# Residual of the last stage partly made by GpSimd, gate and scale applied in one step out of PSUM, last tile in halves

## The reference, cut to what matters

```python
xs = xs + g2s * _peer(h, ...)      # _peer ends in einsum('nhk,nhkd->nd', g * a, v_tab[e])
y_sample = _rmsnorm(xs, norm_final)  # xs * rsqrt(mean(xs*xs) + EPS) * norm_final
```

## Time and profile before

| | |
|---|---|
| median of three runs | 2218.42 us |
| profiled execution, its own time | 2221.55 us |
| its span, first to last instruction | 2219.6 us |
| granted TensorE clock, mean | 0.978 of full speed |
| PE busy | 2110.5 us (95%), 12150 instructions |
| DVE busy | 1781.8 us (80%), 3590 instructions |
| ACT busy | 1240.2 us (56%), 1677 instructions |
| POOL busy | 433.1 us (20%), 408 instructions |

### The profile page before, as it was taken

One profiled execution on the slowest core, in us unless ns is written; L12 is line 12 of the kernel. 1 busy time (PEld: TensorE's weight loads), 2 busy tenths in 40 slices (PEclk: granted clock), 3 DMA queues, 4 the chain that ended last, 5 costly groups with the idle time before them and its releaser, 6 DMA issues. The chain is left out here.

```text
span 2219.6 us, 33667 instructions
## 1 busy us (share of the span) xinstructions
PE 2110.5 (95%) x12150; PEld 1174.3 (53%) x12150; DVE 1781.8 (80%) x3590; ACT 1240.2 (56%) x1677; POOL 433.1 (20%) x408
## 2 busy tenths in 40 slices
PE   6999999978879999999999999999999999999997
PEld 3667676745557744445555554544444444444443
DVE  5467554776776668899999999935999999999999
ACT  4555863465767546524344457766556565565562
POOL 0011110000102200323232333400322222223220
PEclk8999998999999999999999999999999999999998
DMA  7975661008559645788999898995878888888872
GB/s 297 360 289 180 205 205 58 29 11 330 182 184 335 225 163 162 248 271 283 351 305 357 296 350 315 341 373 220 334 291 301 312 296 309 303 301 313 300 268 76
DMA packets 193531, 573.02 MB, mean 258 GB/s; under 512 B 18768, under 2 KB 52336, under 8 KB 186224
## 3 DMA queue, kind: packets, MB, share of 16 engines
q1 hardware_dynamic: 113728, 323.14, 42.4%
q0 software_dynamic: 48704, 173.04, 20.9%
q10 hardware_dynamic: 30960, 75.07, 8.7%
HBM read 454.18 MB, written 117.00 MB: 257 GB/s over the span
## 5 line engine op out<-in xcount | busy, mean ns | idle before, releaser
L307 PE MATMUL mrg_ps<-h_hi,lin_hi 128*128 128x512 f16 (+1 forms) x1376 | 462.2, 359 | 2.8 <-DVE h_lo L640 2.8
L307 PE MATMUL mrg_ps<-h_lo,lin_hi 128*128 128x512 f16 (+1 forms) x1376 | 462.1, 359 | 0.0
L307 PE MATMUL mrg_ps<-h_hi,lin_lo 128*128 128x512 f16 (+1 forms) x1376 | 461.8, 358 | 0.0
L2170 POOL DMA_INDIRECT row<-v_dram,picked x128 | 177.6, 1388 | 559.0 <-DVE acc L2812 438.0
L289 DVE SCALAR_TENSOR_TENSOR lin_lo<-lin_raw,lin_wsc,lin_hi 128x1024 f16<-128x1024 f32 x132 | 169.2, 1282 | 142.5 <-ACT lin_hi L283 142.4
L2234 POOL DMA_INDIRECT row<-u_rows_dram,picked x128 | 175.9, 1374 | 471.9 <-DVE dot_junk L2420 354.0
L283 ACT ACTIVATE lin_hi<-lin_raw,lin_wsc 128x1024 f16<-128x1024 f32 x132 | 151.1, 1146 | 199.5 <-DVE lin_wsc L144 158.2
L2682 PE MATMUL ps_w<-oh_turned,oh_buf 128*128 128x128 f16 x1024 | 224.3, 219 | 5.3 <-ACT region L2348 5.2
L307 PEld LDWEIGHTS mrg_ps<-h_hi,lin_lo 128*128 128x128 f16 x1376 | 135.3, 98 | 128.3 <-issue 1.4
L307 PEld LDWEIGHTS mrg_ps<-h_hi,lin_hi 128*128 128x128 f16 x1376 | 134.5, 98 | 120.5 <-issue 4.2
L307 PEld LDWEIGHTS mrg_ps<-h_lo,lin_hi 128*128 128x128 f16 x1376 | 135.3, 98 | 117.8 <-issue 1.1
(11 more groups left out here) (442 smaller groups left out, 3978.7 us busy)
## 6 DMA issues: line engine op xcount, KB each, us to landing
lin_raw<-w_all_dram SPq DMA_DIRECT2D x132, 512.0 KB, 6.1
act_scratch<-activated ACTq DMA_DIRECT2D x128, 256.0 KB, 4.5
wgt_scratch<-region ACTq DMA_DIRECT2D x64, 512.0 KB, 6.6
region<-v_dram SPq DMA_DIRECT2D x15, 2048.0 KB, 7.8
oh_buf<-v_dram SPq DMA_DIRECT2D x15, 2048.0 KB, 7.7
act_buf<-w_all_dram SPq DMA_DIRECT2D x38, 512.0 KB, 4.3
lin_hi<-split_scratch SPq DMA_DIRECT2D x64, 256.0 KB, 3.4
lin_lo<-split_scratch SPq DMA_DIRECT2D x64, 256.0 KB, 5.0
```

Of the source, the lines that this page charges most:

```text
L307: last = nc.tensor.matmul(self.ps[b % 2][:, half, 0:ts.stop - ts.start], w_[:, kc, :], x_[:, kc, ts], start=(j == 0 and kc == 0), stop=(j ...
L2170: nc.gpsimd.indirect_dma_start(out=row[j % NG][:], out_offset=None, in_=a["v"].rearrange("k (c d) -> (k c) d", d=D), in_offset=bass.Indire ...
```

## The change

GpSimd, after its last row fetch, makes `x2 + acc * gate` for the four latent tiles from the accumulator as it stands before the last group. For each tile it waits until that tile's two add-ups of the group before the last are done. VectorE's tail then handles a tile in two column halves: one step takes the last group's result from PSUM times the scale times the gate row (into `acc`), a second adds it to `x2`. Square sums are made in halves and added. The order of VectorE's tail changes: first half of tile k, variance and the four one-column steps of tile k-1, second half of tile k, normalisation of tile k-1; the last tile's normalisation and store go in two halves.

```diff
--- before.py
+++ after.py
@@ -2722,6 +2722,8 @@
             second.total_ps = pb(c, "ps_tot", [P, 2, 2])
             npass = VGROUPS // 2
             R = 2 * (NLAT // P)
+            BOTH = (slice(0, 512), slice(512, D))
+            FINAL = [(slice(0, D),)] * (NT - 1) + [BOTH]
             upto = [0] + [-(-PICKS * (g + 1) // (VGROUPS - 1)) for g in range(VGROUPS - 1)]
             block = c.enter_context(nc.Block())
 
@@ -2730,6 +2732,14 @@
                 for j in range(NG, PICKS):
                     pool.wait_ge(s("row_add"), j - NG + 1)
                     second_row(j)
+                pool.wait_ge(s("g2"), 4)
+                pool.wait_ge(s("ld7"), 16 * (NT + 1))
+                for k in range(1, NT):
+                    for r in (2 * k - 2, 2 * k - 1):
+                        pool.wait_ge(s(f"y_add{r % YB}"), (2 * R // YB) * (npass - 1) + r // YB + 1)
+                    nc.gpsimd.tensor_tensor(acc[:, k, :], acc[:, k, :], g2row[:, 1, :], ALU.mult).then_inc(s("base"), 1)
+                    pool.wait_ge(s("base"), 2 * k - 1)
+                    nc.gpsimd.tensor_tensor(x2[k][:, :], x2[k][:, :], acc[:, k, :], ALU.add).then_inc(s("base"), 1)
 
             @block.sync
             def _(sp):
@@ -2745,10 +2755,11 @@
                     sp.dma_start(x2[k][:, :], x2_d[k]).then_inc(s("ld7"), 16)
                 run(sp, 2, npass, step)
                 for k in range(NT):
-                    sp.wait_ge(s("final"), k + 1)
                     dst = y_prompt if k == 0 else y_sample[(k - 1) * P:k * P, :]
-                    sp.dma_start(dst, x2[k][:, :]).then_inc(s("st_y"), 16)
-                sp.wait_ge(s("st_y"), 16 * NT)
+                    for n, cs in enumerate(FINAL[k]):
+                        sp.wait_ge(s("final"), k + n + 1)
+                        sp.dma_start(dst[:, cs], x2[k][:, cs]).then_inc(s("st_y"), 16)
+                sp.wait_ge(s("st_y"), 16 * (NT + 1))
 
             @block.scalar
             def _(act):
@@ -2780,12 +2791,14 @@
                     act.wait_ge(s("fin_var"), k + 1)
                     nc.scalar.activation(st[:, 2, k:k + 1], st[:, 1, k:k + 1], ACT.Abs_reciprocal_sqrt).then_inc(s("fin_root"), 1)
                 for k in range(NT):
-                    act.wait_ge(s("resid"), k + 1)
-                    nc.scalar.activation(second.junk[:, 0:D], x2[k][:, :], ACT.Square, accum_out=st[:, 0, k:k + 1]
-                                         ).then_inc(s("ssq"), 1)
-                    act.wait_ge(s("ssq"), k + 1)
-                    if k:
-                        root(act, k - 1)
+                    for n, cs in enumerate(BOTH if k else FINAL[0]):
+                        done = 2 * k + n if k else 1
+                        act.wait_ge(s("resid"), done)
+                        nc.scalar.activation(second.junk[:, cs], x2[k][:, cs], ACT.Square, accum_out=st[:, 3 * n, k:k + 1]
+                                             ).then_inc(s("ssq"), 1)
+                        act.wait_ge(s("ssq"), done)
+                        if k and not n:
+                            root(act, k - 1)
                 root(act, NT - 1)
 
             @block.vector
@@ -2859,48 +2872,65 @@
                         for k in rows if r == R - 1 else (next(rows),) if r % 2 else ():
                             add_row(k)
 
-                def residual(k):
-
-                    if k == 0:
-                        dve.wait_ge(s("row_add"), PICKS)
-                        dve.wait_ge(s("g2"), 4)
-                        dve.wait_ge(s("ld7"), 16 * (NT + 1))
-                    else:
-                        for r in (2 * k - 2, 2 * k - 1):
-                            dve.wait_ge(s(f"y_add{(R + r) % YB}"), (2 * R // YB) * (npass - 1) + (R + r) // YB + 1)
-                    link(V.tensor_tensor(acc[:, k, :], acc[:, k, :], g2row[:, min(k, 1), :], ALU.mult))
-                    V.tensor_tensor(x2[k][:, :], x2[k][:, :], acc[:, k, :], ALU.add).then_inc(s("resid"), 1)
+                def residual_rows():
+
+                    dve.wait_ge(s("row_add"), PICKS)
+                    dve.wait_ge(s("g2"), 4)
+                    dve.wait_ge(s("ld7"), 16 * (NT + 1))
+                    link(V.tensor_tensor(acc[:, 0, :], acc[:, 0, :], g2row[:, 0, :], ALU.mult))
+                    V.tensor_tensor(x2[0][:, :], x2[0][:, :], acc[:, 0, :], ALU.add).then_inc(s("resid"), 1)
+
+                def residual(k, half):
+
+                    r, cs = 2 * k - 2 + half, BOTH[half]
+                    q = R + r
+                    dve.wait_ge(s("vp_y_inv1"), npass)
+                    dve.wait_ge(s("y_mm1"), R * (npass - 1) + r + 1)
+                    dve.wait_ge(s("base"), 2 * k)
+                    V.scalar_tensor_tensor(out=acc[:, k, cs], in0=ps_y[q % YB][:, :], scalar=second.yinv[:, 1:2],
+                                           in1=g2row[:, 1, cs], op0=ALU.mult, op1=ALU.mult).then_inc(s(f"y_add{q % YB}"), 1)
+                    dve.wait_ge(s(f"y_add{q % YB}"), (2 * R // YB) * (npass - 1) + q // YB + 1)
+                    V.tensor_tensor(x2[k][:, cs], x2[k][:, cs], acc[:, k, cs], ALU.add).then_inc(s("resid"), 1)
 
                 def variance(k):
-                    dve.wait_ge(s("ssq"), k + 1)
+                    dve.wait_ge(s("ssq"), 2 * k + 1)
+                    if k:
+                        link(V.tensor_tensor(st[:, 0, k:k + 1], st[:, 0, k:k + 1], st[:, 3, k:k + 1], ALU.add))
                     V.tensor_scalar(st[:, 1, k:k + 1], st[:, 0, k:k + 1], 1.0 / D, EPS, ALU.mult, ALU.add
                                     ).then_inc(s("fin_var"), 1)
 
-                def finish(k):
+                def inverse_root(k):
                     v_, root_, r_, t_ = (st[:, n, k:k + 1] for n in (1, 2, 3, 4))
                     dve.wait_ge(s("fin_root"), k + 1)
                     link(V.tensor_tensor(t_, root_, root_, ALU.mult))
                     link(V.tensor_tensor(t_, t_, v_, ALU.mult))
                     link(V.tensor_scalar(t_, t_, -0.5, 1.5, ALU.mult, ALU.add))
                     link(V.tensor_tensor(r_, root_, t_, ALU.mult))
-                    V.scalar_tensor_tensor(out=x2[k][:, :], in0=x2[k][:, :], scalar=r_, in1=nf[:],
-                                           op0=ALU.mult, op1=ALU.mult).then_inc(s("final"), 1)
+
+                def finish(k):
+                    for cs in FINAL[k]:
+                        V.scalar_tensor_tensor(out=x2[k][:, cs], in0=x2[k][:, cs], scalar=st[:, 3, k:k + 1], in1=nf[:, cs],
+                                               op0=ALU.mult, op1=ALU.mult).then_inc(s("final"), 1)
                 first_group()
                 for i in range(npass):
                     if i:
                         mixed(i, 0, i, 1)
                     if i < npass - 1:
                         mixed(i, 1, i + 1, 0)
-                residual(0)
+                residual_rows()
                 for k in range(1, NT):
-                    add_up(npass - 1, 1, 2 * k - 2)
-                    add_up(npass - 1, 1, 2 * k - 1)
-                    residual(k)
+                    residual(k, 0)
                     variance(k - 1)
+                    if k == 1:
+                        residual(k, 1)
+                    inverse_root(k - 1)
                     if k > 1:
-                        finish(k - 2)
+                        residual(k, 1)
+                    if k < NT - 1:
+                        finish(k - 1)
+                variance(NT - 1)
                 finish(NT - 2)
-                variance(NT - 1)
+                inverse_root(NT - 1)
                 finish(NT - 1)
 
             @block.tensor
```

## The result

| | before | after |
|---|---|---|
| median of the runs timed together | 2218.28 us (4 runs, 2216.62 to 2220.34) | 2234.44 us (4 runs, 2231.47 to 2238.45) |
| profiled execution / its span | 2221.55 / 2219.6 us | 2233.5 / 2231.7 us |
| granted TensorE clock, mean | 0.978 | 0.976 |
| VectorE busy | 1781.8 us, 3590 instructions | 1792.5 us, 3595 instructions |
| GpSimd busy | 433.1 us, 408 instructions | 458.0 us, 416 instructions |

The kernel became slower: ratio 1.0065, interval 1.0053 to 1.0077, which is +11.8 to +17.1 us. The forecast was +13.3 us (2231.7). The two spans differ by 12.1 us; in the profiled execution of after, everything ahead of the last stretch took 1.35 us less. So stretches are compared from a common anchor, the start of the last 2048-column multiply (line 485: 2166.77 before, 2165.42 after).

A forecast was written before the change was run, and what follows sets the result against it. VectorE's full queue was taken to bound the kernel's end. Holds of 13.55 us and -0.2 for the tail and store made +13.3: 2231.7 us for the median, own range 2223.6 to 2239, 8-in-10 range 2217.5 to 2239.

The forecast's parts named there:

- VectorE's queue is the tail: End of kernel: VectorE runs almost without pause from 2187.63 to 2216.58, so each microsecond it loses lengthens the kernel.
- Holds: VectorE from 2170.3: GpSimd's eight SBUF-reading instructions block its two-input steps and line 143, 13.55 us in all.
- the four that were to cost 1.62 behind an add-up: GpSimd instructions entering beside an add-up, holding the second split or a row step behind it: 6.48 us together.
- T: Length of one new GpSimd multiply or add of 128x1024: taken as 2.28 us, between 1.23 and 3.2.
- Who goes next: Back-to-back two-input VectorE steps: a waiting gather was said to wait for the second step too, taking 3.68 us.
- rival 1: VectorE beside GpSimd: its two-input steps go through and only GpSimd waits; -0.2 us, 2218.2; chance 0.24.
- rival 2: VectorE beside GpSimd: instructions interleave, about half the holds, +6.8 - 0.2, 2225.0; chance 0.08 together with rival 4.
- rival 4: Tail: GpSimd starts only there and VectorE waits for each base; +4, 2222; chance 0.08 together with rival 2.
- The tail: VectorE's tail in halves: 27.0 us against 26.55, +0.4, or -0.2 with gaps of 0.03; about 0.8 idle per tile.
- rival 3: Tail: no holds and no new idle time before the inverse root; up to 4 x 0.8 us saved, -3.4, 2215.0; chance 0.05.
- The store: End of kernel: the last store carries 256 KB instead of 512 and saves between nothing and half of 2.6; -0.6 taken.
- up to 6: TensorE before its last group: a hole of up to 6 us from holds ahead of its last split, costing nothing more.

The follow-up runs named there:

- the run with four: The changed kernel with GpSimd making only the four multiplies, not the four adds, against the kernel before: 2229.38 us, ratio 1.0048 (1.003 to 1.0067).

## Why the prediction was right

- **VectorE's queue is the tail.** It held: the +13.67 ahead of the first half, with the tail's +0.30 and the store's -0.5, came out at the end as +13.45. Nothing on the way swallowed it.
- **Holds, 13.55 forecast, 13.58 measured.** The total is nearer than its terms deserve. Line 143 lost 1.82 (1.95 forecast) and the first split 0.73 (0.78). Of the four that were to cost 1.62 behind an add-up, two cost 1.42, and two got in between back-to-back steps and cost 2.07 and 2.08. The residual lost 2.02 twice (2.17 forecast). T was 2.36 undisturbed and about 2.2 from the end of a blocking step, where 2.28 was taken. A held step doesn't begin anew when GpSimd is done: five of them end 1.08 to 1.09 us behind GpSimd's instruction, and not their length of 1.23 to 1.28. So most terms were too large and two too small, and that they cancel is luck. (The 0.33 between the row step's end and line 143 is 0.24 in the rows of both kernels.)
- **Who goes next was misread.** That a waiting gather lets a second back-to-back step pass was taken from the gather at 2124.70. Four others of before, at 1558.01, 1705.65, 1873.82 and 2041.45, also started during a row step with the multiply right behind it, and ended 0.81 to 0.82 behind the row step. Here is one, GpSimd's row and then VectorE's; its row step ends at 2042.57, the gather at 2043.38, and the multiply behind isn't held:

```profile
2041.45 1.93 POOL L2170 DMA_INDIRECT row<-v_dram,picked  x1 [0.92 <-DVE acc L2812]
```

```profile
2039.90 2.67 DVE L2812 SCALAR_TENSOR_TENSOR acc<-row,picked,acc 128x1024 f32<-128x1024 f32 x2
2042.48 2.28 DVE L485 TENSOR_TENSOR eq_buf<-eq_buf,sc_buf 128x2048 f32<-128x2048 f32 x1
```

So the holds of 2.07 and 2.08 could have been expected from the trace of before.
- **Only GpSimd waits (rival 1)** fails: the seven blocked instructions do wait, about 1 us each, but VectorE waits longer, and the kernel without them is at 1.001 (0.9997 to 1.0024). **Shared turns (rival 2)** fails in its price: 13.58 us for the eight where it had 6.8, and 8.02 for four alone. It is right in one thing, that VectorE's next step doesn't go first merely by standing ready.
- **GpSimd in the tail (rival 4)** isn't what happened, and its price of +4 was far too low. The run in which GpSimd starts only there loses as much as after: the prediction had priced VectorE's waits for the base, and not the holds that come with it there.
- **The tail: +0.4 forecast, +0.30 measured.** Idle times of 0.91, three of 0.82, and 0.79 stand where they were put (0.8 each). When the root is moved the three go, and 0.21 is left of the last (**rival 3** had the size right, 3.3 against the forecast 3.2 to 3.4, for another order than the kernel's). The 512-column add was 0.69 for a forecast 0.70; tile 1's 5.80 is as forecast. The gap behind the PSUM step was 0.03 to 0.04, not 0.11, and by the prediction that alone should have given its other end, -0.2. It didn't, in part because the sum holds the gap once in a tile and not twice: its second half runs from t+3.40 to t+4.85, 1.45 us where a half is 1.56.
- **The store:** -0.5 for -0.6. It landed in 2.1 us for 2.6. In the run without GpSimd's part the same half stores took 2.7, so this term is no sure gain.
- **TensorE** had a hole, 4.35 us for "up to 6"; the rest of the holds ahead of it was covered. The prediction left out the granted clock behind the hole. The windows of after show it (length, then PE, PEld, DVE, ACT, POOL busy, clock):

```profile
2184.00:2188.00 4.00, 0.47 (x2) 0.23 (x3) 4.00 (x4) 0.00 (x0) 2.11 (x2) 0.76 0.00 0
2188.00:2192.00 4.00, 4.00 (x11) 1.38 (x10) 4.00 (x3) 0.00 (x0) 3.92 (x2) 0.50 0.00 0
...
2196.00:2200.00 4.00, 4.00 (x20) 1.85 (x19) 3.96 (x2) 0.00 (x0) 3.92 (x2) 1.00 0.00 0
```

In 2188 to 2192 TensorE runs at 0.50, the lower of its two levels (1.2 GHz), with 11 matmuls instead of 20. It cost nothing here: VectorE is full in all these stretches, and at 2203.14 TensorE has waited 2.5 us for VectorE to give back a buffer.

What stays open is the difference of the medians, +16.2, to the +13.45 of the anchor. Single executions of after lie 7 us apart, and the interval (+11.8 to +17.1) holds both; the profiled executions can't say more, as the stretch ahead of the anchor was 1.35 us shorter in after's.

## What to carry to other kernels

An instruction that is given to GpSimd to relieve VectorE was free here only beside VectorE steps that take an operand from PSUM, or where VectorE had slack. So count its VectorE neighbours with two SBUF inputs, and charge each GpSimd instruction that reads SBUF up to its whole length against them (1.4 to 2.1 us of 2.36 where VectorE had no slack). One input is no safeguard: line 143 has one, and lost 1.82. If it must be there, cut it in pieces (8.05 us lost instead of 13.97). And when a tail is one engine's queue, look at where in the queue a result of another engine is first wanted: moving four small steps of each tile was worth 3.3 us in the trace here.

## What the runs showed of the hardware that was not expected

- A GpSimd multiply that comes while VectorE is in a two-input step starts before VectorE's next one, though that stands back to back: the second split and the row step behind lost 2.07 to 2.09 each time (after, and the run with four). Gathers of before did both: the one at 2041.45 got in behind the row step, and the one at 2124.70, which also started during a row step, ended 0.81 after the multiply that followed. Why these two differ wasn't tested.
- The hold doesn't depend on the held step's size. One-column steps of 0.16 with two SBUF inputs took 2.29 beside a GpSimd multiply and 2.00 beside an add, and the two-column line 143 took 1.99.
- Of the steps with one SBUF input, line 143 (two columns) was held, and the one-column step of line 2908 kept 0.15 at 2197.82, beside the add that started at 2197.65 (the run in which GpSimd starts late). What sets line 143 apart wasn't tested.
- A 256-column piece on GpSimd takes 0.72 us undisturbed, 2.9 for four by their sum, where one instruction of 1024 columns takes 2.36.
- A memset on GpSimd, which reads nothing, held line 143 to 0.54 from 0.17, while steps with two inputs, 1024 columns wide, lost nothing beside it.
- Four dependent one-column steps take 1.18 us on ScalarE and 0.76 on VectorE.
